# A stick-breaking attention stage in which TensorE and ScalarE alternate in smaller pieces, and the scan's second operand moves to PSUM

## The reference

```
x += W_o( sig(g_A) * P_A(sparse attention(h)) + sig(g_B) * P_B(stick-breaking(h)) ),  h = RMSNorm(x)
x += ConvGatedMLP(RMSNorm(x));   y = RMSNorm_final(x)
```

```
z = q k^T / 8                                    (strictly causal: key position < query position)
log_keep = log_sigmoid(-z);  after = reverse cumulative sum of log_keep, without the element itself
A = exp(log_sigmoid(z) + after);  out = A v
```

## Time and profile before

| | us |
|---|---|
| median of 3 runs | 2395.78 (2389.12 to 2395.8) |
| the profiled execution | 2393.49 |
| its span, first to last instruction | 2391.5 |
| scores of `stick`: first, and last product with v | 732.8, 927.6 |
| busy in the span: TensorE, VectorE, ScalarE, GpSimd | 2142.7, 1444.0, 766.1, 182.6 |
| 72 scans (L1218), busy | 154.4 |
| 72 weighings (L1071), busy | 164.9 |

### The profile page before, as it was taken

The page is one execution under the profiler, slowest core; times in us unless marked ns, Lnnn a source line. Parts: engine busy times, 40 slices in busy tenths (PEclk is TensorE's granted clock), DMA queues, the critical chain, the costliest instruction groups (busy, mean ns, idle before and its releaser), DMA issues. The chain is left out here.

```text
span 2391.5 us, 36882 instructions
## 1 busy us (share of the span) xinstructions
PE 2142.7 (90%) x13337; PEld 1775.6 (74%) x13337; DVE 1444.0 (60%) x2439; ACT 766.1 (32%) x1421; POOL 182.6 (8%) x120
## 2 busy tenths in 40 slices
PE   4876999999997887887876989899999999999995
PEld 4833888888885555555554878689999999999994
DVE  4448967664587776654443543336656656666566
ACT  4046011111216776664433432222122122122122
POOL 0000000000007884001000000000000000000000
PEclk7988999999999898998998999999999999999997
DMA  4321222232223101540899532021011111111102
GB/s 152 100 50 53 88 84 84 84 119 83 84 69 91 40 29 47 168 163 22 313 356 330 180 116 95 0 75 53 26 53 50 29 53 37 41 53 33 46 21 88
DMA packets 186052, 218.73 MB, mean 91 GB/s; under 512 B 28828, under 2 KB 119324, under 8 KB 184796
## 3 DMA queue, kind: packets, MB, share of 16 engines
q1 hardware_dynamic: 185300, 217.20, 27.7%
q10 hardware_dynamic: 648, 0.15, 0.0%
HBM read 181.17 MB, written 36.13 MB: 91 GB/s over the span
## 5 line engine op out<-in xcount | busy, mean ns | idle before, releaser
L2434 DVE TENSOR_TENSOR x_all<-x_all,ff_down 128x512 f32<-128x512 f32 x396 | 269.9, 688 | 159.3 <-PE ff_down L2338 159.1
L2323 PE MATMUL ff_up<-m_hi,ff_up_hi 128*128 128x368 f32 x1056 | 348.2, 330 | 8.1 <-DVE ff_up_lo L2411 8.1
L2324 PE MATMUL ff_up<-m_lo,ff_up_hi 128*128 128x368 f32 x1056 | 349.0, 331 | 0.0
L2325 PE MATMUL ff_up<-m_hi,ff_up_lo 128*128 128x368 f32 x1056 | 347.3, 329 | 0.0
L419 PE MATMUL pr_acc<-pr_w_hi,h_hi 128*128 128x512 f32 x720 | 281.0, 390 | 16.3 <-DVE pr_w_lo L356 16.3
L420 PE MATMUL pr_acc<-pr_w_lo,h_hi 128*128 128x512 f32 x720 | 280.7, 390 | 0.0
L421 PE MATMUL pr_acc<-pr_w_hi,h_lo 128*128 128x512 f32 x720 | 280.6, 390 | 0.0
L819 DVE TENSOR_SCALAR_CACHE_REDUCE bi_flags<-scores,bi_thr 128x384 bf16<-128x384 f32 (+6 forms) x231 | 215.9, 992 | 1.2
L2323 PEld LDWEIGHTS ff_up<-m_hi,ff_up_hi 128*128 128x128 f32 x1056 | 198.8, 188 | 9.3 <-DVE ff_up_lo L2411 8.5
L2324 PEld LDWEIGHTS ff_up<-m_lo,ff_up_hi 128*128 128x128 f32 x1056 | 198.7, 188 | 0.8
L2325 PEld LDWEIGHTS ff_up<-m_hi,ff_up_lo 128*128 128x128 f32 x1056 | 198.8, 188 | 0.0
(11 more groups left out here) (273 smaller groups left out, 3572.6 us busy)
## 6 DMA issues: line engine op xcount, KB each, us to landing
out_proj<-pr_staged SPq DMA_DIRECT2D x90, 256.0 KB, 2.0
up_raw<-in_w_up SPq DMA_DIRECT2D x44, 512.0 KB, 4.9
w_raw<-in_w_in SPq DMA_DIRECT2D x10, 2048.0 KB, 8.1
sa_keys<-in_cache_k_a SPq DMA_DIRECT2D x64, 256.0 KB, 4.5
sa_values<-in_cache_v_a SPq DMA_DIRECT2D x64, 256.0 KB, 7.6
sa_keys<-in_cache_k_b SPq DMA_DIRECT2D x64, 256.0 KB, 6.5
sa_values<-in_cache_v_b SPq DMA_DIRECT2D x64, 256.0 KB, 5.5
ff_down_raw<-in_w_down SPq DMA_DIRECT2D x22, 512.0 KB, 3.5
```

Of the source, the lines that this page charges most:

```text
L2323: pe.matmul(up[n][:], w, hi[:, c, at], start=c == 0, stop=False)
L2324: pe.matmul(up[n][:], w, lo[:, c, at], start=False, stop=False)
L2325: ins = pe.matmul(up[n][:], w_rest, hi[:, c, at], start=False, stop=c == KC - 1)
L2434: dve.tensor_tensor(at, at, down[n][:], ALU.add).then_inc(down_added.sem, 1)
```

## The change

- TensorE and ScalarE: the new list `woven(n)` cuts the scores of tile n into pairs of chunks (one pair for tiles 0 to 3, two for 4 to 7, three for tile 8) and deals the turned chunks of tile n - 3 out beside them. TensorE makes a pair, then (after the first pair) the use of tile n - 4, then the share of transposes, then the next pair. ScalarE opens a pair and copies that share. The q and k transposes stand after all of it, on both engines.
- The scan's second operand is `unread`, one column in PSUM that is set once and read with a step of zero.
- `unread` takes a PSUM bank, so the output has one bank in place of two: the first tile of a group waits for the evacuation of the group just before it. VectorE evacuates ahead of tile n's scans and no longer behind them.

```diff
@@ stick
-    o = [ctx.enter_context(nc.psum_tensor(f"st_o{b}", [P, 4 * P], F32)) for b in range(2)]
+    o = ctx.enter_context(nc.psum_tensor("st_o", [P, 4 * P], F32))
+    unread = ctx.enter_context(nc.psum_tensor("st_unread", [P, 1], F32))
+    def woven(n):
+
+        beside = turns_of[n - TURN_LAG] if TURN_LAG <= n < NG + TURN_LAG else []
+        if n >= NG:
+            return [(None, beside)]
+        parts, m = len(scores_of[n]) // 2, len(beside)
+        return [(k, beside[k * m // parts:(k + 1) * m // parts]) for k in range(parts)]
@@ TensorE
-                if t == first and b >= 2:
-                    pe.wait_ge(o_out, b - 1)
+                if t == first and b >= 1:
+                    pe.wait_ge(o_out, b)
             for n in range(NG + USE_LAG):
+                for k, chunks_beside in woven(n):
+                    if k is not None:
+                        score(n, k)
+                    if not k and n >= USE_LAG:
+                        use(n - USE_LAG)
+                    for c in chunks_beside:
+                        turn(c)
                 if n < NG:
-                    score(n)
                     i, t = divmod(n, NT)
                     for b in QK_WITH.get(t, ()) if i + 1 < PAIRS else ():
                         turn_qk(i + 1, b)
-                if n >= USE_LAG:
-                    use(n - USE_LAG)
-                if TURN_LAG <= n < NG + TURN_LAG:
-                    turn(n - TURN_LAG)
@@ ScalarE
             for n in range(NG + TURN_LAG):
+                for k, chunks_beside in woven(n):
+                    if k is not None:
+                        open_tile(n, k)
+                    for c in chunks_beside:
+                        take_turn(c)
                 if n < NG:
-                    open_tile(n)
                     i, t = divmod(n, NT)
                     for b in QK_WITH.get(t, ()) if i + 1 < PAIRS else ():
                         take_qk(i + 1, b)
-                if n >= TURN_LAG:
-                    take_turns(n - TURN_LAG)
@@ VectorE
+            dve.memset(unread[:], 1.0).then_inc(unread_set, 1)
+            dve.wait_ge(unread_set, 1)
             for n in range(NG + USE_LAG + 1):
+                if n >= USE_LAG + 1:
+                    i, t = divmod(n - USE_LAG - 1, NT)
+                    if t + 1 == O_GROUPS[group_of[t]][1]:
+                        evacuate(i, group_of[t])
                 if n < NG:
...
-                        dve.tensor_tensor_scan(x[:, ::-1], x[:, ::-1], x[:, ::-1], 1.0, ALU.mult,
-                                               ALU.bypass).then_inc(scanned, 1)
-                if n >= USE_LAG + 1:
-                    i, t = divmod(n - USE_LAG - 1, NT)
-                    if t + 1 == O_GROUPS[group_of[t]][1]:
-                        evacuate(i, group_of[t])
+                        dve.tensor_tensor_scan(x[:, ::-1], x[:, ::-1], unread[0:r, :].to_broadcast([r, w]), 1.0,
+                                               ALU.mult, ALU.bypass).then_inc(scanned, 1)
```

More of the change, by code:

```diff
@@ L1019, in stick @@
     turned = [ctx.enter_context(nc.psum_tensor(f"st_turned{b}", [P, 4, P], F32)) for b in range(NTB)]
-    o = [ctx.enter_context(nc.psum_tensor(f"st_o{b}", [P, 4 * P], F32)) for b in range(2)]
+    o = ctx.enter_context(nc.psum_tensor("st_o", [P, 4 * P], F32))
+    unread = ctx.enter_context(nc.psum_tensor("st_unread", [P, 1], F32))
+    unread_set = sem("unread_set")
     mask_made, mask_stored = sem("mask_made"), sem("mask_stored")
@@ L1086, in turn_qk, with score @@
                 ins.then_inc(made, 1)
-            def score(g):
+            def score(g, k):
                 i, t = divmod(g, NT)
                 r = tile_rows(t)
-                if t == 0:
+                if t == 0 and k == 0:
                     pe.wait_ge(taken, copies_of[i, len(QK) - 1] + 1)
                 last = scores_of[g][-2][0]
-                for c, hh, a, w in scores_of[g]:
+                for c, hh, a, w in scores_of[g][2 * k:2 * k + 2]:
                     if hh == 0:
@@ L1100, in score @@
                         ins.then_inc(made, 1)
-                for c, hh, a, w in scores_of[g][-2:]:
+                for c, hh, a, w in scores_of[g][2 * k:2 * k + 2] if 2 * k + 2 == len(scores_of[g]) else ():
                     at = slice(t * P - a, t * P - a + r)
@@ L1104, in score, with turn @@
                               skip_group_check=True).then_inc(made, 1)
-            def turn(g):
+            def turn(c):
+                g, hh, k0, n = TURNS[c]
                 r = tile_rows(g % NT)
[L1108 to L1118, removed]
+                pe.wait_ge(weighed, 2 * g + hh + 1)
+                if c >= NTB:
+                    pe.wait_ge(turns_out, c - NTB + 1)
+                for j in range(n):
+                    kt = k0 + j
+                    w = tile_rows(kt)
+                    ins = pe.transpose(turned[c % NTB][0:w, j, 0:r], prob[g % R][hh][0:r, kt * P:kt * P + w],
+                                       ident[0:r, 0:r])
+                ins.then_inc(turns, 1)
             def use(g):
@@ L1133, in use @@
                     for hh in range(2):
-                        ins = pe.matmul(o[b % 2][half(hh), at:at + r], v_rows[i % 2][0:w, kt, half(hh)],
+                        ins = pe.matmul(o[half(hh), at:at + r], v_rows[i % 2][0:w, kt, half(hh)],
                                         prob_t[g % 2][hh][0:w, kt, 0:r], start=kt == 0, stop=kt == t,
@@ L1167, in take_qk, with open_tile @@
                 ins.then_inc(taken, 1)
-            def open_tile(g):
+            def open_tile(g, k):
                 r = tile_rows(g % NT)
-                if g >= R:
+                if g >= R and k == 0:
                     act.wait_ge(weighed, 2 * (g - R + 1))
                     act.wait_ge(turns, turns_of[g - R][-1] + 1)
-                for c, hh, a, w in scores_of[g]:
+                for c, hh, a, w in scores_of[g][2 * k:2 * k + 2]:
                     act.wait_ge(made, c + 1)
@@ L1177, in open_tile, with take_turn @@
                     act.activation(prob[g % R][hh][0:r, a:a + w], banks[c % NS][0:r, 0:w], ACT.Sigmoid).then_inc(taken, 1)
-            def take_turns(g):
-                r = tile_rows(g % NT)
-                if g >= 2:
+            def take_turn(c):
+                g, hh, k0, n = TURNS[c]
+                r, w = tile_rows(g % NT), tile_rows(k0)
+                if g >= 2 and c == turns_of[g][0]:
                     act.wait_ge(used, g - 1)
[L1183 to L1188, removed]
+                act.wait_ge(turns, c + 1)
+                act.activation(prob_t[g % 2][hh][0:w, k0:k0 + n, 0:r], turned[c % NTB][0:w, 0:n, 0:r],
+                               ACT.Copy).then_inc(turns_out, 1)
             for b in range(len(QK)):
@@ L1204, in evacuate @@
                 first, last = O_GROUPS[k]
-                b = i * len(O_GROUPS) + k
                 dve.wait_ge(used, i * NT + last)
@@ L1209, in evacuate @@
                 w = min(last * P, NP_ROWS) - first * P
-                dve.tensor_copy(o_all[i % 2][:, first * P:first * P + w], o[b % 2][:, 0:w]).then_inc(o_out, 1)
+                dve.tensor_copy(o_all[i % 2][:, first * P:first * P + w], o[:, 0:w]).then_inc(o_out, 1)
+            dve.memset(unread[:], 1.0).then_inc(unread_set, 1)
+            dve.wait_ge(unread_set, 1)
             for n in range(NG + USE_LAG + 1):
+                if n >= USE_LAG + 1:
+                    i, t = divmod(n - USE_LAG - 1, NT)
+                    if t + 1 == O_GROUPS[group_of[t]][1]:
+                        evacuate(i, group_of[t])
                 if n < NG:
```

## The result

The changed kernel takes 2403.75 us (median of 5 runs, 2403.01 to 2405.74) against 2393.63 us for the kernel before beside it: a ratio of 1.0045, 95% interval [1.003, 1.006], so 10.1 us slower. Forecast were 2398.7 us and a range of 2385 to 2411; slower by over 0.3% had a chance of 0.33, no change 0.50.

A forecast was written before the change was run, and what follows sets the result against it. The prediction took an order of waits between ScalarE and TensorE to bound the stage, no engine being full. Pair terms of +0.3, +1.4 twice and +2.1 gave +5.2 us on 2393.5: 2398.7 us, range 2385 to 2411.

The forecast's parts named there:

- the gap that the forecast is built on: TensorE, each step 8: some 3 us idle before the use of tile 4, until VectorE's copy empties the output bank.
- Part 1: VectorE's scan with second operand in PSUM: 1024-wide scan 2.29 us instead of 3.79, alone saving little.
- Part 2: Pairs of chunks and shares of turned chunks alternate on TensorE and ScalarE: steps 4 to 6 together near 13.8 us.
- Steps 4 to 6: Turns of TensorE's loop, named by the tile whose scores they make: near 13.8 us together in a middle pair.
- Part 3: One output bank instead of two: TensorE stands 3.2 us before the use of tile 4, ScalarE idles 2.9 us.
- steps 7 and 8: TensorE's loop turns for tiles 7 and 8: 17.4 us against 15.7 before, 14.5 without the output-bank wait.
- the rival with the covered wait: Output-bank wait is hidden, so 2.9 us vanish in each of four pairs: 2387 us; chance 0.20.
- The scan still takes turns: VectorE's scan still contends with GpSimd, 2.95 us more in each of four pairs: 2410.5 us; chance 0.12.
- More switching cost than I count: Weights loaded anew and waits at each alternation, 3 us more in the stage and a pair: 2405 us; chance 0.07.
- weave pays in full and the clock stays up: Output wait covered and TensorE's slow stretches go too, some 1.5 us in three pairs: 2382 us; chance 0.11.

The follow-up runs named there:

- e3: Changed kernel without the alternating order, with the output bank evacuated ahead of the scans: 2393.28 us, ratio 0.9997 to the kernel before.
- e2: Kernel before plus only the alternating order, with two output banks and the scan reading itself in SBUF: 2389.19 us, ratio 0.9982 to the kernel before.
- e7: Changed kernel with the output bank emptied one turn earlier, and the scan's second operand again the scanned tile in SBUF: 2388.53 us, ratio 0.9979 to before.
- e8: Changed kernel with the output bank emptied one turn earlier, and the one unread column in SBUF: 2389.92 us, ratio 0.9986 to before.
- e1: Changed kernel with VectorE copying each output group out one turn earlier: 2386.34 us, ratio 0.9968 to the kernel before.
- e6: Changed kernel with TensorE making step 8's second score pair three more times while it would wait for the output bank: 2402.53 us, ratio 1.0037 to before.
- e9: The changed kernel itself, measured once more: 2403.87 us, ratio 1.0045 to the kernel before.
- e10: Changed kernel with four extra output-bank copies ahead of the evacuation, and step 8's second score pair made six more times: 2413.93 us, ratio 1.0081 to before.
- e5: Changed kernel with early evacuation, plus step 8's last q and k transposes and copies ahead of the last share of turned chunks: 2382.22 us, ratio 0.9948 to before.
- e4: Changed kernel with four more copies of the output bank ahead of the evacuation of tiles 0 to 3: 2419.98 us, ratio 1.0101 to before.

## Why the prediction was right

The measured time lies in the range and the gap that the forecast is built on was there in all four pairs. The size was not right: 10.1 us slower where 5 were worked out, and "no change", held likeliest, was not what came.

**The path.** That VectorE and GpSimd don't set the stage's time in the old order: shown by e3, where the wide scans shrink by 40% and the wide products by 50% and the time stays. That the taking turns of TensorE and ScalarE does: shown by e2, where their new order alone saves time.

**Part 1.** A wide scan was put at 2.29 us and took 2.273; the product at 2 and took 1.996. That it saves little alone: e3. That the alternating order with one bank needs it in one place, the prediction did not say: e7 and e8.

**Part 2.** Steps 4 to 6 of a middle pair were put at 13.8 us and took 13.9. Step 7's second pair was to be open 4.3 us after the step's start; it took 4.1 (855.52 to 859.63).

**Part 3.** The step that carries the verdict. From the moment a at which this pair opens (859.63): the use of tile 4 at a + 6.4, measured a + 6.31; the gap 3.2 us, measured 3.07. Its removal (e1) gives 13.9 us for steps 7 and 8 where 14.5 was worked out, and 2386.3 us for the kernel where the rival with the covered wait said 2387.

**The term that was too small.** From the use on, the sum reckoned with full speed: copy of the chunk at a + 8.4, next step 0 at a + 13.1. Measured are a + 9.60 and a + 14.52, and ScalarE idled 4.09 us where 2.9 were worked out. The use took 2.14 instead of 1.31 us and the four transposes 1.12 instead of 0.66 (e1), at 1.2 GHz. With TensorE kept busy (e6) steps 7 and 8 take 17.3 us, the 17.4 of the forecast. So the sum left out that the new standing lowers the clock behind it. It had named the clock only as a chance of gain.

**The sum.** Forecast per pair +0.3, +1.4, +1.4, +2.1, together +5.2 us. Measured in the first profiled execution: 39.3 − 34.4 = +4.9, 52.0 − 50.2 = +1.8, 51.0 − 48.3 = +2.8, 65.8 − 62.0 = +3.8, together +13.2 before rounding; in the repeat (e9) +2.8, +1.1, +2.8, +3.7, together 205.2 − 194.9 = +10.4, close to the 10.1 us of the medians. The first pair differs most between the two (39.3 and 37.2 us): 1.3 us of it lie in steps 0 to 2, which ran at a granted clock of 0.50 in the one and 1.00 in the other, before any gap, and have nothing to do with the change; 0.8 lie in step 8. The terms at the lower clock are 1.4 us from a to the next step 0 (14.52 against 13.1) in each of three pairs, and in the last pair 1.1 us in the use alone (2.40 against 1.31; from step 7 there to the stage's end 33.0 us were worked out and 34.7 measured): some 5 us, half of the loss, which took the result from within 0.3% to over it. The step times of e6 and the stage of e10 bear that out; the time of e6, 1.2 us under the changed kernel where 6 to 8 were expected, does not, so the share stays an account of the profiles and is not shown by a timing.

**The rivals.** "The scan still takes turns" fell with scans of 2273 ns. "More switching cost than I count" named 2405 us, nearer to the result than the forecast's 2398.7, and fell as well: e1 and e2 have all the switching and are faster than before. "Covered wait" did not come true in the change, but describes what e1 reached by another way. That e5 comes to 2382.22 us, the 2382 of "weave pays in full and the clock stays up", is a coincidence: its granted clock over the stage is 0.93, as before, and what it gains comes from another place.

## What to carry to other kernels

An order that brings an engine to a point sooner also brings it sooner to every wait that used to be hidden: for each wait that a change adds, set the moment at which the engine arrives in the new order against the moment of the release, not that of the old order. A buffer given up can be paid for by moving its release one turn earlier, into time in which the releasing engine idles anyway; whether it does idle there depends on the instructions ahead of the release (with slow scans the same early copy came 1.2 us late in one pair). And count a stall of some 3 us on TensorE at more than its length: here part of what came behind ran at half speed each time.

## What the runs showed of the hardware

- Stands of 3.06 to 3.07 us on TensorE, and of 4.68 us in the last pair, were followed in each of the four pairs, in both profiles of the changed kernel, by products at 1.2 GHz (2.1 to 2.4 us for 20 records that take 1.31). So were the stands of 5.46 and 7.07 us in e4. The same gap filled with products whose results nobody reads kept them at 1.31 in all pairs (e6, e10), and shorter stands before the same products, of 1.15 (e1, e2) and of 1.19 to 1.49 us (e7, e8), left them at 1.31 too. With the gap of 5.46 us, filling it made the stage 8.7 us shorter in the profiles and the median 6.1 us lower.
- VectorE's scan contends with GpSimd for as little as one column in SBUF read with a step of zero (3498 ns for 1024 columns), and not at all if that column is in PSUM (2273 ns).
- Open: why, in some profiles of the alternating order, step 0 runs at the slow level (4.5 or 6.0 us) without a long gap ahead of it. No run here tells it.
